# Keys of the latent branch for two heads at a time, its gate behind the transposes, and inverse softmax sums spread by ScalarE and transposed

## The reference, cut to what matters

```python
# latent branch ("mla"): 8 heads, a key has 64 + 32 values, a value 128
q = (rms_norm(qc, q_norm) @ w_uq).reshape(b, n, 8, 64 + 32)
kv = (rms_norm(kvc, kv_norm) @ w_ukv).reshape(b, n, 8, 64 + 128)
k_nope, v = kv[..., :64], kv[..., 64:]          # k = [k_nope, k_rot], k_rot shared by the heads
ya = softmax(q @ k.T * 96**-0.5) @ v            # over 768 keys
# third branch ("swa"): 16 heads of 64, 4 key heads, window of 128 around the query, 256 context keys, a sink
yc = sink_softmax(sink, (s_ctx, s_loc)) @ v
# each branch is gated before its projection
terms.append(sigmoid(gm_r) * ((y_r * silu(z_r)) @ w_branch[r]))
```

## Time and profile before

| | |
|---|---|
| median of 3 runs | 3934.48 us (3934.06 to 3938.59) |
| the profiled execution | 3931.58 us, of which its span 3929.8 us |
| PE busy | 3664.3 us (93% of the span) |
| PEld / DVE / ACT / POOL busy | 2840.4 / 2046.8 / 1404.4 / 259.9 us |
| mean granted clock of TensorE | 0.970 |
| mla, first layer | about 1100 to 1376 us of the span, one head in 32.7 us |
| swa, first layer | about 2160 to 2410 us |
| mla, second layer | about 2725 to 2925 us, one head in 27.3 to 27.6 us |
| swa, second layer | about 3553 to 3773 us |

### The profile page before, as it was taken

How to read it: one execution, slowest core, us unless ns; L and a number is a source line. 1 busy time by engine, 2 the same in 40 slices (tenths; PEclk the granted TensorE clock), 3 DMA queues, 4 the chain that set the end, 5 groups by cost and what they waited for, 6 DMA issues and landing times.

```text
span 3929.8 us, 55394 instructions
## 1 busy us (share of the span) xinstructions
PE 3664.3 (93%) x20467; PEld 2840.4 (72%) x20467; DVE 2046.8 (52%) x3404; ACT 1404.4 (36%) x2502; POOL 259.9 (7%) x196
## 2 busy tenths in 40 slices
PE   5998989999799999999799999998999999799998
PEld 3665768878667788777588776886668777587676
DVE  3565345553545524777634555244453676645644
ACT  2443233332323322444322445122332444424532
POOL 0000000000011001111000100000110211001100
PEclk8998999999899999999899999998999999899999
DMA  7453335543101122111122111211103222131122
GB/s 255 146 140 89 88 91 161 165 145 103 44 22 29 30 64 59 46 51 44 31 59 57 41 28 49 67 57 41 39 27 94 62 58 65 37 88 51 42 73 80
DMA packets 502211, 286.96 MB, mean 73 GB/s; under 512 B 43753, under 2 KB 481093, under 8 KB 502062
## 3 DMA queue, kind: packets, MB, share of 16 engines
q1 hardware_dynamic: 481010, 263.63, 23.9%
q10 hardware_dynamic: 21052, 21.33, 1.7%
HBM read 269.05 MB, written 10.32 MB: 71 GB/s over the span
## 4 chain that ended last, share of the span: by engine, by line
issue 90%; PE 3%; POOL 3%; POOLq 2%; DVE 1%; ACT 0%; DVEq 0%; ACTq 0%
PE ps L604 3%; POOLq L1332 2%; POOL qT L1331 2%; POOL qT L1333 1%; POOL y_and_merged L1331 1%; DVEq L2810 0%; DVE w_low L600 0%; DVE probs L883 0%; PE ps L1030 0%; PE ps L2321 0%; POOLq L211 0%; DVE h_low L2143 0%; DVE y_and_merged L2787 0%; DVE y_low L2575 0%; ACT w_high L590 0%
## 5 line engine op out<-in xcount | busy, mean ns | idle before, releaser
L604 PE MATMUL ps<-h_high,w_high 128*128 128x512 f32 (+1 forms) x3432 | 1281.9, 374 | 42.8 <-DVE w_low L600 18.7
L604 PE MATMUL ps<-h_low,w_high 128*128 128x512 f32 (+1 forms) x3432 | 1245.8, 363 | 0.0
L604 PE MATMUL ps<-h_high,w_low 128*128 128x512 f32 (+1 forms) x3432 | 1242.7, 362 | 0.0
L604 PEld LDWEIGHTS ps<-h_high,w_high 128*128 128x128 f32 x3432 | 651.4, 190 | 207.3 <-issue 63.2
L600 DVE TENSOR_TENSOR w_low<-w_raw,w_high 128x1024 fp32r<-128x1024 f32 x374 | 455.9, 1220 | 602.3 <-ACT w_high L590 580.7
L604 PEld LDWEIGHTS ps<-h_high,w_low 128*128 128x128 f32 x3432 | 652.0, 190 | 103.2
L604 PEld LDWEIGHTS ps<-h_low,w_high 128*128 128x128 f32 x3432 | 652.8, 190 | 93.1 <-issue 2.6
L590 ACT ACTIVATE w_high<-w_raw 128x1024 fp32r<-128x1024 f32 x374 | 387.8, 1038 | 643.4 <-PE ps L604 543.4
L862 ACT ACTIVATE probs<-ps,neg_max 128x768 f32<-128x768 f32 (+1 forms) x240 | 194.5, 814 | 431.1 <-DVE neg_max L894 431.0
L604 PE MATMUL ps<-probsT,v 128*128 128x512 f32 (+4 forms) x736 | 286.6, 560 | 13.6 <-DVE probsT L1093 8.6
L894 DVE TENSOR_REDUCE neg_max<-ps 128x1 f32<-128x768 f32 (+1 forms) x240 | 196.5, 846 | 168.6 <-PE ps L604 157.5
(11 more groups left out here) (238 smaller groups left out, 4042.1 us busy)
## 6 DMA issues: line engine op xcount, KB each, us to landing
w_raw<-in_w_in SPq DMA_DIRECT2D x436, 256.0 KB, 3.2
y_and_merged<-in_w_mod SPq DMA_DIRECT2D x96, 256.0 KB, 3.1
w_raw<-in_w_branch SPq DMA_DIRECT2D x96, 256.0 KB, 3.0
w_raw<-in_w_up SPq DMA_DIRECT2D x88, 256.0 KB, 4.2
y_and_merged<-in_w_ada SPq DMA_DIRECT2D x64, 256.0 KB, 3.3
w_raw<-in_w_out SPq DMA_DIRECT2D x48, 256.0 KB, 3.0
w_raw<-in_w_down SPq DMA_DIRECT2D x44, 256.0 KB, 2.9
y_and_merged<-in_w_ada SPq DMA_DIRECT2D x4, 2048.0 KB, 19.9
```

Of the source, the lines that this page charges most:

```text
L604: return nc.tensor.matmul(*a, **kw)
```

## The change

Three things are changed.

1. **Pairs of keys.** The key columns of heads 2t and 2t + 1 are loaded as one operand of 128 columns (two more DMAs a pair, semaphore `s_pair`), and the key projection ahead of an even head (`opens_pair`) makes 128 rows in place of 64. ACT copies the odd head's 64 rows from PSUM to `KB` (two instructions), and then evacuates the even head's as before. Ahead of an odd head PE makes no key projection; ACT makes `KH` from `KB` (one 64x768), DVE `KL` (one 64x768).
2. **A later gate.** In the steps of even heads (0, 2, 4, 6) `mla_side` gives the next head's queries first and then z, and `NO_KEYS` leaves a longer tail of side units behind the last item (8 of 22 in the first layer, 5 of 11 in the second). The gate's parts on ACT (w_high, tanh) come behind its evacuation of chunk 1, on DVE w_low behind chunk 2 and the gate behind chunk 4. In the steps of odd heads the order stays as it was.
3. **Inverse sums of swa.** ACT widens the inverses to 64 columns each by one activation with a broadcast operand, behind its evacuation of chunk 1, and PE transposes them 128 columns at a time, 4 transposes (and 2 for the context) for both heads at once. In the second layer they go to another bank, and the next pair's scores wait for `y` instead of `z_scaled`.

The core of the diff:

```diff
+                        if u == 0:
+                            for kc in range(2):
+                                pair = wukv[l][:, kc, bass.ds(i * 192, 384)].rearrange("p (a m) -> p a m", m=192)[:, :, 0:64]
+                                sp.dma_start(WN[:, slot(s, "n", u), 544 + 128 * kc:672 + 128 * kc].rearrange("p (a m) -> p a m", m=64), pair).then_inc(s_pair, 16)
...
+        NO_KEYS = {16 + 6: 8, 8 + 3: 5}
...
-                return min(max(n_side - TAIL, 0) * (group + 1) // (groups - 1), max(n_side - TAIL, 0))
+                tail = NO_KEYS.get(n_side, TAIL)
+                return min((n_side - tail) * (group + 1) // (groups - 1), n_side - tail)
...
-                if i:
+                if i and s["cq"]:
                     pe.wait_ge(S["z_scaled"], cnt(s, "z_scaled", t, per, u))
                 else:
-                    pe.wait_ge(S["y"], s.base["y"])
+                    pe.wait_ge(S["y"], cnt(s, "y", t, per, u - 1 if i else 0))
...
+        def act_wide(act, s, t, u, i):
+
+            act.wait_ge(S["normed"], cnt(s, "normed", t, 1, u + 1))
+            n = s["items"]
+            act.activation(wide_inverses(s, i).rearrange("p (a b) -> p a b", b=64), RL[:, 0:n].unsqueeze(2).to_broadcast([128, n, 64]), ACT.Copy)\
+               .then_inc(S["rl_wide"], 1)
...
-                for j in range(heads):
-                    idx = heads * qt + j
-                    dst = 4 * 512 + 128 * qt if qt < 4 else out_banks(i)[1] * 512 + 256 + 128 * (qt - 4)
-                    last = mm(PS[64 * j:64 * j + m, dst:dst + 128], RL[:, idx:idx + 1].to_broadcast([128, m]), ident[:, :], start=True, stop=True,
-                              skip_group_check=True)
+                dst = bank(inverse_bank(s, i), 128, 128 * qt) if qt < 4 else bank(out_banks(i)[1], 128, 256 + 128 * (qt - 4))
+                last = nc.tensor.transpose(dst, wide_inverses(s, i)[:, 128 * qt:128 * qt + 128], ident[:, :])
...
+                if not opens_pair(s, u):
+                    return
...
-                for lo, n, ps in tgroups(2, True, 64):
+                pe.wait_ge(s_pair, 32 * t + 32 * (s.base["kv_ev"] + 1))
+                for lo, n, ps in tgroups(2, True):
                     for kc in range(2):
-                        last = mm(ps, WN[:, k, 288 + 192 * kc:288 + 192 * kc + 64], M[:, 3 + kc, lo:lo + n], start=kc == 0, stop=kc == 1)
+                        last = mm(ps, WN[:, k, 544 + 128 * kc:672 + 128 * kc], M[:, 3 + kc, lo:lo + n], start=kc == 0, stop=kc == 1)
...
+                if not opens_pair(s, u):
+                    act.activation(KH[0:64, :], KB[0:64, 0, :], ACT.Copy).then_inc(S["rope_in"], 1)
+                    return
...
+                for lo, n in ((0, LAT), (LAT, CTX)):
+                    act.activation(KB[0:64, 0, lo:lo + n], PS[64:128, 1024 + lo:1024 + lo + n], ACT.Copy)
...
             def mla_side(t, u, i):
+                if u % 2 == 0:
+                    yield from qk_steps(pe, nxt, t, u, i + 1, True)
                 yield from mla_z(t, u, i)
-                yield from qk_steps(pe, nxt, t, u, i + 1, True)
+                if u % 2:
+                    yield from qk_steps(pe, nxt, t, u, i + 1, True)
...
+                        if c == 1 and name == "mla" and u % 2 == 0:
+                            act_proj_z(act, s, t, u, i)
...
+                    if name == "mla" and u % 2 == 0:
+                        if c == 2:
+                            dve_low(dve, s, t, 2, u + 1)
+                        if c == 4:
+                            dve_gate(dve, s, t, u)
```

More of the change, by code:

```diff
@@ L180, in plan @@
             if s["name"] == "mla":
-                add(s, q_mm=n, q_out=n, kv_ev=n, kv_low=n, v_ev=n, z_ev=n, tanh=n, swap_q=32 * n, roped=n)
+                add(s, q_mm=n, q_out=n, kv_ev=n // 2, kv_low=n, v_ev=n, z_ev=n, tanh=n, swap_q=32 * n, roped=n)
             if s["name"] == "diff":
@@ L184, in plan @@
             if s["name"] == "swa":
-                add(s, z_ev=n, tanh=n, swap_q=64 * n, roped=n, z_scaled=n)
+                add(s, z_ev=n, tanh=n, swap_q=64 * n, roped=n, z_scaled=n, rl_wide=n)
         elif k == "merge":
@@ L949, in dve_softmax, with inverse_bank, wide_inverses, spread_inverses @@
                 normalise(n - 1)
-        def spread_inverses(pe, s, t, u):
-            pe.wait_ge(S["normed"], cnt(s, "normed", t, s["unroll"], u + 1))
-            spread(s, range(4), u).then_inc(S["rl_mm"], 1)
+        def inverse_bank(s, i):
+            return 4 if s["cq"] else out_banks(i)[1]
+        def wide_inverses(s, i):
+            n = s["items"] * 64
+            return KB[:, 0, 0:n] if i == 7 else Y[:, 7, 0:n]
+        def act_wide(act, s, t, u, i):
[3 more added lines that the diff above has]
+               .then_inc(S["rl_wide"], 1)
+        def spread_inverses(pe, s, t, u, i):
+            pe.wait_ge(S["rl_wide"], cnt(s, "rl_wide", t, s["unroll"], u + 1))
+            spread(s, range(4), i).then_inc(S["rl_mm"], 1)
         def spread_context(pe, s, i):
@@ L1104, in program, with opens_pair @@
         SCALE = {"dil": 0.125, "na": 0.125, "mla": 96.0 ** -0.5, "diff": 0.125, "swa": 0.125}
+        def opens_pair(s, u):
+            return (u + (1 if s["moved"] else 0)) % 2 == 0
         def qk_steps(pe, s, t, u, i, ahead):
@@ L1161, in qk_steps, with side_plan @@
                 yield from split_steps(pe, s, t, s["nh"], 1, 128, tgroups(2, not s["first"]))
-        def side_plan(s):
+        def side_plan(s, u=0):
             q = {"mla": 3}.get(s["name"], 8) * (2 if s["cq"] else 1)
-            k = {"mla": 4, "swa": 0}.get(s["name"], 8 if s["first"] else 16)
+            k = {"mla": 4 if u % 2 else 0, "swa": 0}.get(s["name"], 8 if s["first"] else 16)
             size = 2 if paired(s) else 1
@@ L1193, in v_steps @@
                     for kc in range(2):
-                        last = mm(ps, M[:, 3 + kc, lo:lo + 128], WN[:, k, 288 + 192 * kc + 64:288 + 192 * kc + 192], start=kc == 0, stop=kc == 1)
+                        last = mm(ps, M[:, 3 + kc, lo:lo + 128], WN[:, k, 288 + 128 * kc:416 + 128 * kc], start=kc == 0, stop=kc == 1)
                     if lo < 640:
@@ L1355, in dve_proj_qk @@
                 dve.wait_ge(S["rope_in"], cnt(s, "rope_in", t, ui, u + 1))
+                if not opens_pair(s, u):
+                    nc.vector.tensor_tensor(KL[0:64, :], KB[0:64, 0, :], KH[0:64, :].bitcast(F32), ALU.subtract).then_inc(S["kv_low"], 1)
+                    return
                 for d, p in evac_cols(s, 2, KL, True, slice(0, 64)):
@@ L1518, in moved @@
             m = Stage(s.kind, **s.p)
+            m.p["moved"] = True
             m.base = dict(s.base)
@@ L1693, in mla_z @@
             def mla_z(t, u, i, idx):
-                if idx == z_group(s):
+                if u % 2 and idx == z_group(s, u):
                     act_proj_z(act, s, t, u, i)
@@ L1744, in step, with between @@
                     act_proj_qk(act, nxt, t, u, i + 1)
-                    evac_twin(act, s, t, u, i, 0, lambda c: act_qk_high(act, nxt, t, u, i + 1) if c == 5 else None)
+                    def between(c):
+                        if c == 1:
+                            act_wide(act, s, t, u, i)
+                        if c == 5:
+                            act_qk_high(act, nxt, t, u, i + 1)
+                    evac_twin(act, s, t, u, i, 0, between)
                     return
```

26 lines of the change are left out of this document (15 added, 11 removed).

## The result

The changed kernel took 3912.35 us (median of 4 runs, 3908.44 to 3915.06), the kernel before 3935.52 us beside it (4 runs, 3934.06 to 3938.59): a ratio of 0.9939 with an interval of 0.9924 to 0.9954, that is 23 us less (18 to 30). Forecast were 3903 and 31.8 us less. The direction was right, the time lies in the range, and about a quarter of the gain is missing.

The account below looks back on a forecast made before the run. PE, busy 93% of the span, was taken as the bound, with waits on DVE outside the first latent branch. 10.9 + 14.4 − 1.2 + 3.2 + 4.5 = 31.8 us off 3934.5 gave 3903 us; range 3890 to 3920.

Parts of the forecast that it names:

- first rival: Second layer's heads and swa's joints: DVE's chain sets them, removed waits return, only products count: 3914 us; 13%.
- Pairs of keys, first layer: Latent branch, first layer: four of eight heads lose a key projection of 2.73 us each, 10.9 us, no stall.
- 0.3 for v instead of 0.2: Even steps, both layers: first query product waits for the copy of v, 0.2 us a head, 1.2 us against.
- second rival: Odd steps: ACT's copies of the pair are on the path, 8 x 0.7 = 5.6 us, 3908; 7%.
- Second layer: Latent branch, second layer: four joints lose the key projection and two waits, about 3.6 us each, 14.4 us.
- 4 x 3.6: Second layer's latent branch: 2.73 + 0.54 + 0.26, about 3.6 us, won at each of four joints, 14.4 us.
- swa, first layer: Joints of swa's first layer: transposes replace spread products, 0.45 us at four, 0.3 at three, 0.5 at the end: 3.2 us.
- swa, second layer: Joints of swa's second layer: scores wait for low parts alone; 4 x 0.5 + 3 x 0.7 + 0.4 = 4.5 us.
- The 3.48 us of the earlier trace: PE idle time in a swa stretch at granted clock 0.81; its clock fall, 1.3 us, might go (low end).
- Each fits with 0.7 us over: Values phase: w_high, tanh, w_low and gate fit idle time ahead of evacuations on ACT and DVE, costed at nothing.
- fourth rival: Values phase becomes bound by evacuation, moved work lies on the path: slower, 3945 us; 5%.
- third rival: swa pairs: the clock falls behind the transposes, 1.3 us in each of 16 pairs, 21 us, 3924; 5%.

Follow-up runs that it names:

- Early_gate: Changed kernel with pairs of keys kept, but z first, the gate amid the exponents and only 2 or 3 query units behind the last scores: 3929.97 us (0.9990).
- again_2: The changed kernel, unchanged, timed and traced once more: 3908.89 us (0.9936).
- shifted: Changed kernel plus ten unread one-column products at the end of the first layer's latent prologue, which also move the PE code behind them: 3908.98 us (0.9932).
- Warm: Changed kernel plus unread 512-column products, 2 in the first layer and 3 in the second, at the end of the latent prologue: 3903.54 us (0.9920).
- latent_only: Changed kernel with the third branch (swa's inverse sums) put back as before: 3913.30 us (0.9940).
- again: The changed kernel, unchanged, in another series: 3907.66 us (0.9924).
- double_low: Changed kernel with w_low made twice in the values phase of even heads: 3925.57 us in one run.

## Why the prediction came out as it did

The median of 3912 lies in the range, but nearer to the first rival's 3914 than to 3903; which of the two mechanisms holds is read from the heads and joints.

**Pairs of keys, first layer: right.** Forecast 4 x 2.73 less 3 x 0.2 = 10.3 us; measured 9.4 to 9.5 in every run of this code. Even heads inside the stage take 30.20 against 32.70, with 0.3 for v instead of 0.2. Odd heads take 32.52, 0.18 less than before: the copies of the pair, the second rival, are not on the path. Early_gate shows the reason to be the right one: with the shorter cover the same missing product wins nothing. From head 0's first scores to head 7's the gain is 10.9 us; 1.4 of it is lost again in head 7's values phase. Its first product in after and before:

```profile
1352.77 2.08 PE L609 MATMUL ps<-probsT,v 128*128 128x512 f32 x2 [2.19 <-DVE probsT L1112]
```

```profile
1357.38 1.13 PE L604 MATMUL ps<-probsT,v 128*128 128x512 f32 x2 [2.19 <-DVE probsT L1093]
```

The wait is the same, but in after the granted clock is 0.50 from 1352.3 to 1355.7, and in before it is 1.00. Nine of the eleven traces with pairs of keys have this fall, neither of the two without them has it; why is open. It is a loss that the prediction did not look for.

**Second layer: mechanism right, one head of four mis-sized.** The even heads inside the stage take 23.79, 23.77 and 23.69 us against 27.27, 27.28 and 27.19, 3.5 less each; 3.6 less 0.2 was forecast (2.73 + 0.54 + 0.26 is 3.53, so 14.1 in all and not 14.4), and the first rival had 2.73. First scores of heads 2 and 3, after and before:

```profile
2788.94 0.47 PE L609 MATMUL ps<-k_high,q_high 96*128 96x512 f32 x1
2812.73 0.48 PE L609 MATMUL ps<-k_high,q_high 96*128 96x512 f32 x1
```

```profile
2788.91 0.47 PE L604 MATMUL ps<-k_high,q_high 96*128 96x512 f32 x1
2816.18 0.47 PE L604 MATMUL ps<-k_high,q_high 96*128 96x512 f32 x1
```

The step "4 x 3.6" failed at head 0, which won 0.8 (2.1 in again_2, 2.2 in shifted): its score phase opens at the low clock. The prediction read joints inside the stage and took the first head for one of them; what comes ahead of it, an idle time for the first query, had not been read. Warm restores it. Shifted and latent_only lose 1.8 us in head 7's values phase here, at a clock of 0.50 as in the first layer, which is why their stages show 11.4 and 11.5.

**swa, first layer: the term that was mis-sized, 1.2 to 1.4 instead of 3.2.** Two readings were wrong. Four transposes were taken as a quarter of the 1.91 us of 16; they cost 0.59 from their start to the next product. After and before, the same joint inside a key head, on PE:

```profile
2183.25 0.65 PE L609 MATMUL ps<-probsT,v 128*64 128x256 f32 x4
2183.83 0.66 PE L987 MATMUL ps<-ident,y_and_merged 128*128 128x128 f32 x4
2184.42 0.65 PE L609 MATMUL ps<-y_and_merged,v 128*64 128x256 f32 x4
2185.00 0.44 PE L987 MATMUL ps<-ident,y_and_merged 128*128 128x128 f32 x2
2185.39 0.38 PE L609 MATMUL ps<-k_high,q_high 64*128 64x256 f32 x2
```

```profile
2185.15 0.65 PE L604 MATMUL ps<-probsT,v 128*64 128x256 f32 x4
2185.63 1.04 PE L604 MATMUL ps<-ident,exp_sum_inv 128*64 128x128 f32 x16
2186.51 0.60 PE L604 MATMUL ps<-y_and_merged,v 128*64 128x256 f32 x4
2186.94 0.61 PE L604 MATMUL ps<-ident,exp_sum_inv 128*64 128x128 f32 x8
2187.59 0.39 PE L604 MATMUL ps<-k_high,q_high 64*128 64x256 f32 x2
```

From the first of these products to the scores 2.44 us became 2.14, 0.30 where 0.45 was taken. The spread itself gave 0.29 and the context 0.26, but a product ahead of a transpose lasts 0.58 to the next start, and ahead of the spread it lasted 0.48 and 0.43. Both prices stood in the trace of before, 0.58 for four transposes and 0.58 for the product ahead of the next ones:

```profile
2256.71 0.66 PE L1030 MATMUL ps<-ident,y_and_merged 128*128 128x128 f32 x4
2257.29 0.65 PE L604 MATMUL ps<-y_and_merged,v 128*64 128x256 f32 x4
2257.87 0.66 PE L1030 MATMUL ps<-ident,y_and_merged 128*128 128x128 f32 x4
```

At the three joints with a new key head 0.07 was won instead of 0.3, because PE waits there for the last evacuation, which stands on DVE behind both low parts:

```profile
2297.68 0.65 PE L609 MATMUL ps<-y_and_merged,v 128*64 128x256 f32 x4 [0.78 <-DVE y_and_merged L1095]
```

```profile
2296.25 0.95 DVE L1344 TENSOR_TENSOR k_low<-y_and_merged,k_high 128x768 fp32r<-128x768 f32 x1
2297.12 0.42 DVE L1095 COPY y_and_merged<-ps 128x256 f32<-128x256 f32 x1
```

The wait before was 0.49 at this place; the transposes made PE earlier and the wait longer. This is the first rival's mechanism ("each wait that I strike out comes back as another one"), in one stage only. The packets of instructions took some 3 us more, with the score phase behind the longest joint, in two of three traces.

**swa, second layer: right.** All seven joints are 0.70 us shorter (10.76 to 10.05, 12.36 to 11.65), 4.9 together against 4.1 in the terms; the score phases give back 0.1 each, the last one 0.5 (14.41 for 13.86). The 3.48 us of the earlier trace rows was itself a joint with a packet of instructions at 2.8 us, 13.74 against 12.36, and 1.36 more in the score phase behind it, which took 17.11 for 15.75. Without a packet there after gets that back too, but one of its own score phases, that of pair 6, takes 17.28 with the granted clock at 0.50 from 3704.0 to 3707.5; *again*, with two packets and two such phases, loses most of the gain.

**What I called free: right in its result, wrong in its reason.** "Each fits with 0.7 us over" held on ACT (0.91) and not on DVE (0). So the point from which the values phase is bound by evacuation, the fourth rival's, was one operation away and not 0.7 us: double_low crossed it. The third rival rested on the Trainium skill, "TensorE: Matmul & The Clock Gate", Part 4, by which transposes do not count for the clock as products do. No run here shows a cost of that. The score phases behind the transposes in swa's first layer take 23.1 to 23.2 us, as before, except behind three joints that a packet met (23.9 in after and again, 24.3 in double_low). In the second layer the granted clock fell to 0.50 eight times in the score phases of the eleven traces with these transposes, and once in each of the two traces without them.

**The sum.** Against 31.8 the stages lose 0.8 and 2.0 in the latent branch, 1.9 in swa's first layer and some 3 more where a packet met it; swa's second layer gives 1.9 back, and the rest is the stray of executions in code that no edit touches. The 1.3 us between the stages is lost in after, again, latent_only and shifted, where the granted clock is 0.50 for 37.5 us of that stretch, and hardly in warm, where it is so for 30.7 us, as in before. But again_2 has 37.5 us as well and loses nothing, so the reason stays open.

## What to carry to other kernels

A product that is removed may have been the cover of a chain on another engine: look for the chain's end ahead of the next instruction, and move other work into its place, as z's tail here; without it 22 us shrink to next to nothing. Take the price of a short group from a group of that length, with the step into it and out of it, never as a share of a long one. Read the first turn of a loop by itself: here an idle time ahead of it cost clock in its first microseconds, which a few unread products won back.

## What the runs showed of the hardware

- A packet of 16 KB with instructions, when it starts 1.7 to 3.5 us after the first of four swaps in a joint, came with a joint 0.54 to 1.83 us longer (15 of 15; of the 139 others none by more than 0.03).
- A subtraction of 128 x 1024 on VectorE with two operands in SBUF took 1.22 us alone and 2.03 beside a step of the rotation on POOL, which went from 1.26 to 2.06; each ended 1.08 to 1.12 us behind the end of the other engine's instruction before it, so they took turns.
- Behind 4 us with 0.20 us of PE's work the granted clock of the next 6 us was 0.50; with three unread products in that gap it was 1.00, and the head there took 23.48 us instead of 26.49.
